# Retention values as a fifth seven-product unit, and three gate tiles ahead of the mix stage

## The chip, the cores and the metric

The kernel runs on one core of a Trainium2 chip. The metric is the time of one execution on the device in microseconds (us). One profiled execution gives the trace that is read here. The engines are named as the profile does: PE is TensorE (matrix products), DVE is VectorE, ACT is ScalarE, POOL is GpSimd, SP is SyncE, which here only issues transfers.

## The reference

Two layers run over 512 tokens of width 1024, in fp32. Each layer is a half-step SwiGLU, a mixer, and another half-step SwiGLU:

```
x = x + 0.5 * swiglu(rmsnorm(x, norm_ffn1[l]), ...)
h = rmsnorm(x, norm_mix[l]);  z = h @ w_in[l]
rq, rk, rv, rg, dq, dk, dv, g_ret, g_dil = split(z)
y_ret = retention(rq, rk, rv, rg, ...) @ w_ret_o[l]
y_dil = dilated_attention(dq, dk, dv, ...) @ w_dil_o[l]
gates = sigmoid(concat(g_ret, g_dil) + b_gate[l])
x = x + (gates[:, :1024] * y_ret + gates[:, 1024:] * y_dil) @ w_out[l]
x = x + 0.5 * swiglu(rmsnorm(x, norm_ffn2[l]), ...)
```

The change concerns `z = h @ w_in`, the projection of the mixer. Its column groups are rq and rk (512 each), rv and rg (1024 each), dq, dk and dv (1536 each), and the two gates g_ret and g_dil (1024 each).

## The kernel before

**Arithmetic.** An fp32 product is made of three faster products: each operand is split into a high part (`hi`, rounded, written by ACT) and a low part (`lo`, the rest, a subtraction on DVE), and `three` (L692 to L694) issues hi·hi, hi·lo and lo·hi. So every weight that PE uses passes a transfer on SP's queue into `raw`, an ACT copy into `ring_hi` and a DVE subtraction into `ring_lo`. PE waits for the last by the semaphore `weights_lo`. A tile of 128 by 512 results over the full depth of 1024 is 24 matmuls of 512 columns.

**The mixer of a layer** runs in this order. First the *cover*: plain blocks of z, 512 columns each, two units of weights (`cols512`) per block and four tiles of 24 matmuls per unit pair. There are three blocks, `C_DQ` (first third of dq) and two of `C_RV` (rv). While PE works on them, the other engines prepare the stage: `add_squares` on DVE (L1813, L1815) adds the squares of x, `norm_sums` on PE sums them, `norm_factor` on DVE makes the reciprocal root, `norm_spread` on PE spreads it, then DVE forms the normed input `xn` (L2308) and its sums, and `mix_operand` splits these operands (ACT L1551, DVE L2246).

Then the *stage*: the rest of dq, all of dk and dv, in four units. A unit computes 1024 columns over a 2 by 2 blocking with seven products in place of eight (`stage_product`, 24 matmuls each). DVE makes four sums of weight blocks for it (`stage_t1` to `stage_t4`, L2259, L2265, L2268), ACT and DVE split seven operands of 128x2048 (`stage_hi` L1565, `stage_lo` L2252), and the results are combined by DVE and ACT from eight PSUM banks. SP loads the weight blocks (`st_block`, L385) behind waits for earlier splits (`split_of`).

Then four *heads*, each with eight tiles of z: rq and rk, four gate tiles (two of g_ret, two of g_dil, ended by `gate_sigmoid` L1497), two tiles of rg (ended by `gate_silu` L1503). Between the matmuls of these tiles PE does the attention and retention of the head, at places written by hand in `between`: a dictionary per tile says before which of the tile's eight matmul triples a step goes. The steps that matter here: `move` (`dil_move`, L980) waits for `st_spread` of DVE (L2124); `rs(3)`, the last score product, is read by `ret_decay` (L2188); `kq(0)` to `kq(5)` (`qk_turn`, L1062) transpose the next head's q and k and are copied out by `qk_turned_copy` (`turned`, ACT L1519). `kq(2)` waits for `k_scaled` of DVE's `qk_scale` (L2237), behind `ret_decay(3)`, `qk_factors` (nine small operations) and `scores_lo(3)`. `rope` (L2167) reads the banks of the first two tiles. The results of the head before are finished in the next one by `ret_normed`, `ret_gated`, `ret_low` on DVE and `ret_out` on ACT (L1534).

Every engine runs its instructions in the order in which its own function issues them; semaphores join the engines. The *merge* and the second SwiGLU follow. In layer 0 the cover lies at 358.9 to 425.4 us of the span, the stage up to 577, the heads up to 834.5 and the merge up to 941. Layer 1 has the same order 1279.9 us later.

## Time and profile before

| | us |
|---|---|
| median of three runs | 2577.52 |
| lowest and highest | 2577.41, 2577.7 |
| the profiled execution | 2577.28 |
| its span, first to last instruction | 2575.5 |
| busy: PE | 2567.7 |
| busy: DVE | 1936.4 |
| busy: ACT | 1121.0 |

The profiled execution lasts 1.8 us longer than its span and is 0.2 us below the median. An engine's busy time is the time in which it executes an instruction. The views below are a list of PE's waits and timelines: a timeline row gives the start in us from the start of the span, the length, the engine, the line of kernel.py, the operation with output and inputs, and in brackets the idle time ahead of it and what ended that.

### The profile page before, as it was taken

How to read it: one execution, taken by the hardware profiler on the slowest of the kernel's cores; microseconds unless marked ns; L12 is line 12 of the kernel's file. 1: busy time of each engine (PE TensorE's matmuls, PEld its weight loads, DVE VectorE, ACT ScalarE, POOL GpSimd, SP SyncE). 2: the span in 40 equal slices, each digit the busy share in tenths (PEclk: the TensorE clock that was granted, in tenths of full speed). 3: DMA queues.
4: the chain of work that ended last, by engine and by line, in shares of the span. 5: the costliest groups of instructions: out<-in, count | busy, mean ns of one | idle time of the engine just before them, and what ended most of it. 6: DMA issues, size and time to landing. Idle time of an engine off the chain costs nothing.

```text
span 2575.5 us, 36835 instructions
## 1 busy us (share of the span) xinstructions
PE 2567.7 (100%) x14577; PEld 2255.3 (88%) x14577; DVE 1936.4 (75%) x2430; ACT 1121.0 (44%) x1369; POOL 128.5 (5%) x199
## 2 busy tenths in 40 slices
PE   9999999999999999999999999999999999999999
PEld 7999988888888888999989999888888888889998
DVE  8877866886776679777788777777867766797776
ACT  5433444445655234333443334454466642343332
POOL 1111000110001000000000000011100000000000
PEclk9999999999999999999999999999999999999999
DMA  5433245545443433333223332454554434333331
GB/s 183 150 124 119 66 141 191 175 161 175 138 139 115 164 103 119 103 102 98 99 83 123 98 98 74 173 178 147 172 155 139 138 128 151 115 115 98 103 107 52
DMA packets 201202, 328.98 MB, mean 128 GB/s; under 512 B 15572, under 2 KB 122497, under 8 KB 200525
## 3 DMA queue, kind: packets, MB, share of 16 engines
q1 hardware_dynamic: 186312, 286.35, 34.9%
q0 software_dynamic: 14112, 36.50, 3.9%
q10 hardware_dynamic: 646, 4.31, 0.4%
q8 instruction: 89, 1.46, 0.2%
q14 instruction: 43, 0.35, 0.0%
HBM read 289.11 MB, written 42.64 MB: 129 GB/s over the span
## 4 chain that ended last, share of the span: by engine, by line
PE 99%; DVE 0%; DMA 0%; issue 0%; ACT 0%; ACTq 0%
PE proj L692 23%; PE proj L694 23%; PE proj L693 23%; PE acc L693 9%; PE acc L692 9%; PE acc L694 9%; PE acc L1062 1%; PE acc L988 1%; PE acc L1011 0%; PE acc L970 0%; PE acc L971 0%; PE acc L972 0%; PE acc L1001 0%; PE acc L1000 0%; PE acc L765 0%; PE acc L759 0%
## 5 line engine op out<-in xcount | busy, mean ns | idle before, releaser
L692 PE MATMUL proj<-h_hi,ring_hi 128*128 128x256 f32 (+1 forms) x1632 | 553.4, 339 | 1.8 <-DVE h_lo L1791 1.8
L694 PE MATMUL proj<-h_hi,ring_lo 128*128 128x256 f32 (+1 forms) x1632 | 544.6, 334 | 0.0
L693 PE MATMUL proj<-h_lo,ring_hi 128*128 128x256 f32 (+1 forms) x1632 | 543.7, 333 | 0.0
L692 PE MATMUL proj<-y_hi,ring_hi 128*128 128x256 f32 (+1 forms) x1472 | 450.5, 306 | 0.0
L694 PE MATMUL proj<-y_hi,ring_lo 128*128 128x256 f32 (+1 forms) x1472 | 450.5, 306 | 0.0
L693 PE MATMUL proj<-y_lo,ring_hi 128*128 128x256 f32 (+1 forms) x1472 | 450.5, 306 | 0.0
L1262 ACT ACTIVATE ring_hi<-raw 128x1024 fp32r<-128x1024 f32 (+1 forms) x175 | 209.9, 1203 | 360.3 <-PE acc L694 194.6
L692 PEld LDWEIGHTS proj<-h_hi,ring_hi 128*128 128x128 f32 x1632 | 310.3, 190 | 31.4 <-DVE ring_lo L2572 2.2
L694 PEld LDWEIGHTS proj<-h_hi,ring_lo 128*128 128x128 f32 x1632 | 309.9, 190 | 31.2
L693 PEld LDWEIGHTS proj<-h_lo,ring_hi 128*128 128x128 f32 x1632 | 310.4, 190 | 27.5
L692 PEld LDWEIGHTS proj<-y_hi,ring_hi 128*128 128x128 f32 x1472 | 281.3, 191 | 12.5
L694 PEld LDWEIGHTS proj<-y_hi,ring_lo 128*128 128x128 f32 x1472 | 281.3, 191 | 12.5
L693 PEld LDWEIGHTS proj<-y_lo,ring_hi 128*128 128x128 f32 x1472 | 281.2, 191 | 12.4
L1834 DVE TENSOR_TENSOR ring_lo<-raw,ring_hi 128x1024 fp32r<-128x1024 f32 (+1 forms) x176 | 249.0, 1415 | 51.3 <-ACT ring_hi L1262 50.5
L692 PE MATMUL acc<-y_hi,ring_hi 128*128 128x512 f32 x640 | 249.3, 390 | 0.0
L693 PE MATMUL acc<-y_lo,ring_hi 128*128 128x512 f32 x640 | 249.2, 389 | 0.0
L694 PE MATMUL acc<-y_hi,ring_lo 128*128 128x512 f32 x608 | 236.5, 389 | 0.0
L1223 ACT ACTIVATE ring_hi<-raw 128x2048 fp32r<-128x2048 f32 x64 | 122.5, 1913 | 156.7 <-PE proj L694 88.5
L1783 DVE TENSOR_TENSOR ring_lo<-raw,ring_hi 128x2048 fp32r<-128x2048 f32 x64 | 146.3, 2286 | 52.0 <-ACT ring_hi L1223 51.7
L692 PEld LDWEIGHTS acc<-y_hi,ring_hi 128*128 128x128 f32 x640 | 120.2, 188 | 24.5
L693 PEld LDWEIGHTS acc<-y_lo,ring_hi 128*128 128x128 f32 x640 | 120.2, 188 | 24.3
L694 PEld LDWEIGHTS acc<-y_hi,ring_lo 128*128 128x128 f32 x608 | 114.1, 188 | 23.9
(335 smaller groups left out, 4309.6 us busy)
## 6 DMA issues: line engine op xcount, KB each, us to landing
raw<-in_w_in SPq DMA_DIRECT2D x120, 512.0 KB, 4.7
raw<-in_ffn_gate SPq DMA_DIRECT2D x88, 512.0 KB, 3.7
raw<-in_ffn_up SPq DMA_DIRECT2D x88, 512.0 KB, 4.3
raw<-in_ffn_down SPq DMA_DIRECT2D x56, 512.0 KB, 4.4
qkv_d<-work POOLq DMA_DIRECT2D x72, 256.0 KB, 2.6
work<-in_ffn_down SPq DMA_DIRECT2D x32, 512.0 KB, 5.9
xs<-qkv_d SPq DMA_DIRECT2D x24, 512.0 KB, 6.3
xs<-in_w_in SPq DMA_DIRECT2D x16, 512.0 KB, 5.2
```

Source lines behind the costliest of these rows:

```text
L692: pe.matmul(o, s_hi, m_hi, start=start, stop=False, skip_group_check=onto)
L693: pe.matmul(o, s_hi, m_lo, start=False, stop=False, skip_group_check=onto)
L694: return pe.matmul(o, s_lo, m_hi, start=False, stop=stop, skip_group_check=onto)
L988: last = pe.transpose(AB[i % 2][:, c * P:(c + 1) * P], s_t[i][:, c * P:(c + 1) * P], ident[:, :])
L1062: last = pe.transpose(bank[:, b * P:(b + 1) * P], xs[:, x, b * P:(b + 1) * P], ident[:, :])
L1223: act.activation(w_hi[u.slot][:, 0:n], raw[:, u.slot, 0:n], ACT.Copy).then_inc(weights_hi, 1)
L1262: act.activation(ring_hi[:, slot * PIECE:slot * PIECE + words], source, ACT.Copy).then_inc(weights_hi, 1)
L1783: dve.tensor_tensor(w_lo[u.slot][:, 0:n], raw[:, u.slot, 0:n], w_hi[u.slot][:, 0:n].bitcast(fp32), ALU.subtract).then_inc(weights_lo, 1)
L1834: dve.tensor_tensor(ring_lo[:, c], source, ring_hi[:, c].bitcast(fp32), ALU.subtract).then_inc(weights_lo, 1)
```

## The change

Per layer, the two `C_RV` blocks leave the cover, and rv becomes a unit of the stage, the first of now five. Three gate tiles of g_dil (`COVER_GATES`: 2, 4, 6) leave the heads 1, 2 and 3 and are computed in the cover behind the dq block, in the banks AB[2], AB[3] and PB[0]; DVE scales them (`cover_scale`), ACT takes the sigmoid (`cover_sigmoid`), POOL stores them. In matmuls of 512 columns the cover goes from 288 to 168, the stage from 672 to 840, the heads from 768 to 696. In the cover `norm_sums` moves from behind the first unit's four tiles to behind its second tile, and `norm_spread` from inside the second unit to its start. The heads 1 to 3 have seven tiles, and the tiles of all heads use banks by a table (`HEAD_BANKS`): the fifth tile of head 0 goes from PB[2] to PB[1]. The steps between the tiles are placed anew: in the heads 1 to 3, 15 matmuls lie between the last of `rs(3)` and `kq(2)`, where there were 27. On DVE `ret_normed`, `ret_gated` and `ret_low` go to the end of the head, on ACT `ret_out`, `ret_copy` and both `gate_silu` go behind `turned(5)`.

```diff
-COVER_BLOCKS, ST_UNITS = 3, 4
-ST_BASE = 2 * COVER_BLOCKS
+ST_BASE, ST_UNITS = 5, 5
+COVER_TILES = (NB, NB, 1, 1, 1)
+COVER_GATES = (2, 4, 6)
...
+HEAD_TILES = ((2, 2, 2, 2), (2, 2, 1, 2), (2, 2, 1, 2), (2, 2, 1, 2))
...
-ST_COLS = (C_DK, C_DQ + 4 * P, C_DK + 4 * P, C_DQ + 8 * P, C_DK + 8 * P, C_DV, C_DV + 4 * P, C_DV + 8 * P)
+ST_COLS = (C_RV, C_RV + 4 * P, C_DK, C_DQ + 4 * P, C_DK + 4 * P, C_DQ + 8 * P, C_DK + 8 * P, C_DV, C_DV + 4 * P, C_DV + 8 * P)
...
+        HEAD_BANKS = ((0, 1, 2, 3, 1, 2, 3, 0), (1, 2, 3, 0, 1, 2, 3), (0, 1, 2, 3, 0, 1, 2), (3, 0, 1, 2, 3, 0, 1))
...
             def cover(l):
+                item, N = unit(l, 0).index, 3 * l + 1
+                cols512(unit(l, 0), win_v, l, C_DQ, 0)
+                cols512(unit(l, 1), win_v, l, C_DQ, 4)
+                sp.dma_start(cos_r[:, :], c_cos).then_inc(rope_in, 16)
+                sp.dma_start(sin_r[:, :], c_sin).then_inc(rope_in, 16)
+                col128(unit(l, 2), win_v, l, C_GD + COVER_GATES[0] * P)
+                sp.wait_ge(ssq_added, 3 * (N + 1))
+                st_block(l, st_b22[0], 4, ST_COLS[1], b22_landed[0])
+                sp.wait_ge(norm_sum, N + 1)
+                st_block(l, st_b12[0], 0, ST_COLS[1], b12_landed)
+                col128(unit(l, 3), win_v, l, C_GD + COVER_GATES[1] * P)
+                col128(unit(l, 4), win_v, l, C_GD + COVER_GATES[2] * P)
                 split_of(item + ST_BASE - 2)
                 st_block(l, st_b11, 0, ST_COLS[0], b11_landed)
                 split_of(item + ST_BASE - 1)
...
             def cover(l):
                 N = 3 * l + 1
-                for i in range(ST_BASE):
-                    u, part, blk = unit(l, i), i % 2, i // 2
+                for part in (0, 1):
+                    u = unit(l, part)
                     begin(u)
                     for b in range(NB):
-                        if part == 0 and blk:
-                            pe.wait_ge(cover_copied, NB * (COVER_BLOCKS * l + blk - 1) + b + 1)
                         for k in range(4):
                             kt, c = 4 * part + k, k * SEQ
-                            if blk == 0 and b == 0:
+                            if b == 0:
                                 pe.wait_ge(h_lo_ready, 8 * N + kt + 1 + FREE)
                             last = three(PB[b][:, :], h_hi[:, kt, b * P:(b + 1) * P], h_lo[:, kt, b * P:(b + 1) * P],
                                          w_hi[u.slot][:, c:c + SEQ], w_lo[u.slot][:, c:c + SEQ], kt == 0, kt == KT - 1)
                         last.then_inc(tiles_done, 1)
-                        if i == 1 and b == 1:
-                            norm_spread(N)
-                    if i == 0:
-                        norm_sums(N)
+                        if part == 0 and b == 1:
+                            norm_sums(N)
+                    if part == 0:
+                        norm_spread(N)
+                for b, bank in enumerate((AB[2], AB[3], PB[0])):
+                    u = unit(l, 2 + b)
+                    begin(u)
+                    if b == 2:
+                        pe.wait_ge(cover_copied, COPIED * l + 1)
+                    tile_cols(u, bank, 0, width=P)
...
-                    between = ({2: [scores(0), scores(1)]}, {0: [scores(2), scores(3)], 1: [total]}, {2: [move]}, {},
-                               {0: [turn(0), turn(1)], 5: [turn(2), turn(3), values(0), values(1)]},
-                               {1: [values(2), values(3), near_values], 5: [rs(0)]})
-                between += ({0: [rs(1)], 1: [kq(0)], 3: [rv(0), rs(2)], 5: [kq(1)], 6: [rv(1), rs(3)]},
-                            {0: [rv(2)], 3: [rv(3), kq(2)], 4: [kq(3)], 6: [kq(4)], 7: [kq(5)]})
-                banks = PB[0:4] + PB[2:4] + PB[0:2]
-                st = 2 * ST_UNITS * l + 2 * ST_UNITS - 1 + BANK
+                    between = ({2: [scores(0), scores(1)]}, {0: [scores(2), scores(3)], 1: [total]}, {2: [move]},
+                               {2: [turn(0), turn(1)], 7: [turn(2), turn(3), values(0), values(1)]},
+                               {3: [values(2), values(3), near_values], 7: [rs(0)]})
+                if n == 0:
+                    between += ({0: [rs(1)], 1: [kq(0)], 3: [rv(0), rs(2)], 5: [kq(1)], 6: [rv(1), rs(3)]},
+                                {0: [rv(2)], 3: [rv(3), kq(2)], 4: [kq(3)], 6: [kq(4)], 7: [kq(5)]})
+                else:
+                    between += ({2: [rs(1)], 3: [kq(0)], 5: [rv(0), rs(2)], 6: [kq(1)]},
+                                {0: [rv(1), rs(3)], 2: [rv(2)], 3: [kq(2)], 4: [kq(3)], 5: [rv(3)], 6: [kq(4)], 7: [kq(5)]})
...
             def cover(l):
                 split(unit(l, 1))
-                split(unit(l, 2))
-                cover_out(l, 0, 0)
-                cover_out(l, 0, 1)
                 norm_copy(3 * l + 1)
-                cover_out(l, 0, 2)
-                cover_out(l, 0, 3)
-                split(unit(l, 3))
+                split(unit(l, 2), KT * P)
+                cover_out(l, 0)
+                cover_out(l, 1)
+                cover_out(l, 2)
                 mix_operand(l, 0)
+                cover_out(l, 3)
+                split(unit(l, 3), KT * P)
                 mix_operand(l, 1)
-                split(unit(l, 4))
-                for b in range(NB):
-                    cover_out(l, 1, b)
                 mix_operand(l, 2)
-                split(unit(l, 5))
+                split(unit(l, 4), KT * P)
                 stage_hi(l, 0, 0)
                 stage_hi(l, 0, 1)
-                for b in range(NB):
-                    cover_out(l, 2, b)
+                cover_sigmoid(l, 0)
+                cover_sigmoid(l, 1)
+                cover_sigmoid(l, 2)
...
                 squares(2, 4)
                 scores_hi(H, n, 1)
                 turned(0)
+                squares(4, 6)
+                scores_hi(H, n, 2)
+                turned(1)
+                split(at(4))
+                scores_hi(H, n, 3)
+                turned(2)
+                turned(3)
+                turned(4)
+                ret_squares(H, 0)
+                ret_squares(H, 1)
+                turned(5)
+                gate_silu(H, 0, at(3).tile)
                 if n:
                     ret_out(H - 1, n - 1, 0)
                     ret_out(H - 1, n - 1, 1)
-                squares(4, 6)
-                split(at(4))
-                scores_hi(H, n, 2)
-                turned(1)
-                scores_hi(H, n, 3)
-                gate_silu(H, 0, at(3).tile)
-                turned(2)
-                turned(3)
-                ret_squares(H, 0)
-                ret_squares(H, 1)
-                turned(4)
                 ret_copy(H, n, 0)
                 ret_copy(H, n, 1)
-                turned(5)
                 gate_silu(H, 1, at(3).tile + 1)
...
+            def cover_scale(l, b):
+                done(unit(l, 2 + b).tile)
+                dve.wait_ge(cover_stored[b], 16 * (2 * l + 1))
+                dve.tensor_tensor(cover_gate[b], (AB[2], AB[3], PB[0])[b][:, :], r_b[:, :], ALU.mult).then_inc(sxn_ready, 1)
...
                 add_squares(N)
                 split(unit(l, 1))
                 norm_factor(N)
-                split(unit(l, 2))
                 dve.wait_ge(r_ready, N + 1)
-                for m in range(KT):
-                    dve.scalar_tensor_tensor(xn[:, m, :], xs[:, m, :], pars[l][:, R_N[1] + m:R_N[1] + m + 1], r_b[:, :],
-                                             ALU.mult, ALU.mult).then_inc(sxn_ready, 1)
-                dve.wait_ge(sxn_ready, KT * (l + 1))
-                dve.tensor_tensor(s_acc, xn21, xn22, ALU.add).then_inc(sum_ready, 1)
-                split(unit(l, 3))
+                normed(NB, KT)
+                split(unit(l, 2), KT * P)
+                normed(0, NB)
+                dve.wait_ge(sxn_ready, SXN * l + KT)
+                dve.wait_ge(x_spilled, 16 * (l + 1))
+                dve.tensor_tensor(s_sum, xn21, xn22, ALU.add).then_inc(sum_ready, 1)
                 dve.tensor_tensor(s_diff, xn11, xn21, ALU.subtract).then_inc(sum_ready, 1)
                 mix_operand(l, 0)
                 dve.wait_ge(sum_ready, 4 * l + 1)
-                dve.tensor_tensor(s_acc, xn11, s_acc, ALU.subtract).then_inc(sum_ready, 1)
+                dve.tensor_tensor(s_sum, xn11, s_sum, ALU.subtract).then_inc(sum_ready, 1)
+                split(unit(l, 3), KT * P)
                 mix_operand(l, 1)
-                split(unit(l, 4))
                 mix_operand(l, 2)
                 dve.wait_ge(sum_ready, 4 * l + 3)
-                dve.tensor_tensor(s_acc, xn12, s_acc, ALU.add).then_inc(sum_ready, 1)
-                split(unit(l, 5))
+                dve.tensor_tensor(s_sum, xn12, s_sum, ALU.add).then_inc(sum_ready, 1)
+                split(unit(l, 4), KT * P)
                 stage_t1(l, 0)
                 stage_t3(l, 0)
                 stage_lo(l, 0, 0)
+                cover_scale(l, 0)
+                cover_scale(l, 1)
                 stage_t2(l, 0)
                 stage_lo(l, 0, 1)
+                cover_scale(l, 2)
...
                     ret_factor(H - 1)
-                    ret_normed(H - 1)
                 split(at(3))
-                if n:
-                    ret_gated(H - 1)
                 dil_out(H, n)
...
-                if n:
-                    ret_low(H - 1, n - 1)
                 ret_decay(H, 2)
                 reduce(4)
                 scores_lo(H, n, 2)
                 reduce(5)
-                split(at(4))
                 ret_decay(H, 3)
                 if more:
                     qk_factors(H + 1)
                 scores_lo(H, n, 3)
                 if more:
                     qk_scale(H + 1)
+                split(at(4))
+                if n:
+                    ret_normed(H - 1)
+                    ret_gated(H - 1)
+                    ret_low(H - 1, n - 1)
```

In the cover DVE's order around the stage's first operands is this. `y_lo` and `h_lo` are the low parts of mix operands, `ring_lo` those of weights; `raw<-xs,raw` and its like are the weight sums. Before:

```order
L2321 TENSOR_TENSOR work<-work 128x1024
L1783 TENSOR_TENSOR ring_lo<-raw,ring_hi 128x2048
L2259 TENSOR_TENSOR raw<-xs,raw 128x2048
L2265 TENSOR_TENSOR xs<-xs 128x2048
L2252 TENSOR_TENSOR ring_lo<-raw,ring_hi 128x2048
L2268 TENSOR_TENSOR raw<-raw,xs 128x2048
L2252 TENSOR_TENSOR ring_lo<-xs,ring_hi 128x2048
L2252 TENSOR_TENSOR ring_lo<-raw,ring_hi 128x2048
L2246 TENSOR_TENSOR h_lo<-work,h_hi 128x4x256 x2
L2246 TENSOR_TENSOR y_lo<-work,y_hi 128x1024
L2246 TENSOR_TENSOR h_lo<-work,h_hi 128x4x256 x2
L2252 TENSOR_TENSOR ring_lo<-raw,ring_hi 128x2048
```

Of the change (L2322 is `mix_operand`, L2328 `stage_lo`, L2335 `stage_t1`, L2341 `stage_t3`, L2344 `stage_t2`, L2379 `cover_scale`):

```order
L2335 TENSOR_TENSOR raw<-work,raw 128x2048
L2341 TENSOR_TENSOR work<-work 128x2048
L2328 TENSOR_TENSOR ring_lo<-raw,ring_hi 128x2048
L2379 TENSOR_TENSOR xs<-acc,r_b 128x512 x2
L2344 TENSOR_TENSOR raw<-raw,work 128x2048
L2328 TENSOR_TENSOR ring_lo<-work,ring_hi 128x2048
L2379 TENSOR_TENSOR xs<-proj,r_b 128x512
L2328 TENSOR_TENSOR ring_lo<-raw,ring_hi 128x2048
L2322 TENSOR_TENSOR h_lo<-work,h_hi 128x4x256 x2
L2322 TENSOR_TENSOR y_lo<-xs,y_hi 128x1024
L2322 TENSOR_TENSOR h_lo<-work,h_hi 128x4x256 x2
L2328 TENSOR_TENSOR ring_lo<-raw,ring_hi 128x2048
```

The sums and splits keep their order among themselves; three scalings of gate tiles (L2379) now lie between them.

At the end of head 1 ACT's order is as follows, from the first `gate_silu` (L1503) to the first exponential of head 2 (L1446). L1519 is `turned`, here (2) to (5), L1524 `ret_squares`, L1529 `ret_copy`, L1223 a split. Before:

```order
L1503 ACT_TABLE_LOAD
L1503 ACTIVATE work<-proj 128x512
L1519 ACTIVATE xs<-acc,gqs 128x4x8x16
L1519 ACTIVATE xs<-acc,params 128x4x8x16
L1524 ACTIVATE work<-acc 128x512 x2
L1519 ACTIVATE xs<-acc,params 128x512
L1529 ACTIVATE work<-acc,params 128x512 x2
L1519 ACTIVATE xs<-acc,params 128x512
L1503 ACTIVATE work<-proj 128x512
L1223 ACTIVATE ring_hi<-raw 128x2048
L1446 ACT_TABLE_LOAD
L1446 ACTIVATE work,raw<-work,raw 128x128
```

Of the change, from `turned(3)` on (L1578 `turned`, L1583 `ret_squares`, L1562 `gate_silu`, L1593 `ret_out`, L1588 `ret_copy`, L1502 the exponentials):

```order
L1578 ACTIVATE xs<-acc,params 128x4x8x16
L1578 ACTIVATE xs<-acc,params 128x512
L1583 ACTIVATE work<-acc 128x512 x2
L1578 ACTIVATE xs<-acc,params 128x512
L1562 ACT_TABLE_LOAD
L1562 ACTIVATE work<-proj 128x512
L1593 ACTIVATE y_hi<-work 128x512 x2
L1588 ACTIVATE work<-acc,params 128x512 x2
L1562 ACTIVATE work<-proj 128x512
L1279 ACTIVATE ring_hi<-raw 128x2048
L1502 ACT_TABLE_LOAD
L1502 ACTIVATE work,raw<-work,raw 128x128
```

The table load with the first `gate_silu`, and the two `ret_out`, which stood ahead of `turned(2)`, now stand behind `turned(5)`, and so do the two `ret_copy`; `ret_squares` went from ahead of `turned(4)` to behind it. `ret_out` is followed on DVE by `ret_low`, for which `ret_copy` waits.

## Rows read from the trace of the kernel before

**Rows 1.** All waits of PE: who waited for whom, us in total, times, longest.
```profile
PE acc L1205 <- DVE ones_r L2525: 2.8, 1, 2.8
PE proj L692 <- DVE h_lo L1791: 1.8, 1, 1.8
```

**Rows 2.** Span and mean granted TensorE clock of the core.
```profile
core 0: 2575.5 us, clock 1.000
```

**Rows 3.** Timeline of PE, layer 0, cover: start us, us, engine, line, operation.
```profile
358.90 0.39 PE L692 MATMUL proj<-ring_hi,h_hi 128*128 128x512 f32 x1
...
364.34 0.39 PE L692 MATMUL proj<-ring_hi,h_hi 128*128 128x512 f32 x1
```

**Rows 4.** Timeline of DVE, layer 0, start of the cover.
```profile
364.83 0.69 DVE L1815 TENSOR_TENSOR work<-work 128x512 f32<-128x512 f32 x1
```

**Rows 5.** Timeline of DVE, layer 0, cover.
```profile
388.58 1.22 DVE L2246 TENSOR_TENSOR y_lo<-work,y_hi 128x1024 fp32r<-128x1024 f32 x1
389.72 1.22 DVE L2316 TENSOR_TENSOR work<-work 128x1024 f32<-128x1024 f32 x1
...
417.42 2.28 DVE L2268 TENSOR_TENSOR raw<-raw,xs 128x2048 f32<-128x2048 f32 x1
419.62 2.28 DVE L2252 TENSOR_TENSOR ring_lo<-xs,ring_hi 128x2048 fp32r<-128x2048 f32 x1
```

**Rows 6.** Timeline of ACT, layer 0, cover.
```profile
405.05 1.05 ACT L1551 ACTIVATE y_hi<-work 128x1024 fp32r<-128x1024 f32 x1
406.00 1.91 ACT L1223 ACTIVATE ring_hi<-raw 128x2048 fp32r<-128x2048 f32 x1
```

**Rows 7.** Tile raw, 399 to 424 us: its loads' times to landing.
```profile
DMA to landing us min/median/max: 3.7/4.4/4.9
```

**Rows 8.** Issues of line 385: duration ns min/median/max, first and last start.
```profile
L385 SPq DMA_DIRECT2D raw<-in_w_in x32: 367/419/510, 399.2 to 1803.3; - x32
```

**Rows 9.** Timeline of PE, head 0 of layer 0, start of its fifth tile.
```profile
607.38 0.47 PE L692 MATMUL proj<-h_hi,ring_hi 128*128 128x512 f32 x1
607.69 0.39 PE L693 MATMUL proj<-h_lo,ring_hi 128*128 128x512 f32 x1
```

**Rows 10.** Timeline of DVE, head 0 of layer 0.
```profile
608.23 0.68 DVE L2167 TENSOR_TENSOR work<-proj,cos_sin 128x512 f32<-128x512 f32 x1
```

**Rows 11.** Timeline of ACT, head 0 of layer 0.
```profile
605.25 1.28 ACT L1497 ACT_TABLE_LOAD   x1
606.55 0.69 ACT L1497 ACTIVATE r_b<-proj,params 128x512 f32<-128x512 f32 x1
```

**Rows 12.** Timeline of PE, end of head 1 of layer 0.
```profile
693.88 0.39 PE L694 MATMUL acc<-ring_lo 128*128 128x512 f32 x1
...
704.79 0.60 PE L1062 MATMUL acc<-ident,xs 128*128 128x128 f32 x4
```

**Rows 13.** Timeline of DVE, end of head 1 of layer 0.
```profile
694.31 0.69 DVE L2188 SCALAR_TENSOR_TENSOR work<-acc,raw 128x512 f32<-128x512 f32 x1 [0.48 <-PE acc L694]
...
699.73 0.68 DVE L2188 SCALAR_TENSOR_TENSOR work<-acc,raw 128x512 f32<-128x512 f32 x1
...
702.88 1.22 DVE L2237 TENSOR_TENSOR xs<-xs,q_rqk 128x1024 f32<-128x1024 f32 x1
```

**Rows 14.** Timeline of ACT, end of head 1 and start of head 2.
```profile
710.12 0.69 ACT L1519 ACTIVATE xs<-acc,params 128x512 f32<-128x512 f32 x1
710.69 0.61 ACT L1503 ACTIVATE work<-proj 128x512 f32<-128x512 f32 x1
...
714.81 0.40 ACT L1446 ACTIVATE work<-work,raw 128x128 f32<-128x128 f32 x1 [0.41 <-DVE raw L2118]
...
716.63 0.51 ACT L1446 ACTIVATE work<-work,raw 128x256 f32<-128x256 f32 x1 [0.84 <-DVE raw L2118]
```

**Rows 15.** Timeline of DVE, start of head 2.
```profile
724.90 0.23 DVE L2124 TENSOR_TENSOR raw<-raw 128x64 f32<-128x64 f32 x1 [0.64 <-ACT work L1446]
```

**Rows 16.** Timeline of PE, start of head 2.
```profile
726.47 0.30 PE L980 MATMUL acc<-raw 128*128 128x32 f32 x2
```

More of the change, by code:

```diff
@@ L109, in piece_tile @@
 def piece_tile(layer, u, j):
-    return layer * TILES_LAYER + FFN_TILES + NB * ST_BASE + 2 * (PROD * u + j)
+    return layer * TILES_LAYER + FFN_TILES + sum(COVER_TILES) + 2 * (PROD * u + j)
 def ffn_item(layer, f):
@@ L376, in two_cols128, with col128 @@
                          (v[:, :, :, P:2 * P], w[:, ds(layer, 1), :, ds(col1, P)])])
+            def col128(u, w, layer, col):
+                v = slot(u, KT * P).rearrange("p o (k c) -> p o k c", c=P)
+                load(u, [(v[:, :, k:k + 4, :], w[:, ds(layer, 1), k:k + 4, ds(col, P)]) for k in (0, 4)])
             def cols512(u, w, layer, col, k0=0):
@@ L1502, in gate_silu @@
                     act.wait_ge(ret_y, 4 * H)
-                act.activation(silu[:, e, :], PB[e][:, :], ACT.Silu).then_inc(silu_ready, 1)
+                n = H % RET_HEADS
+                bank = head_bank(n, 2 + len(head_gates(n)) + e)
+                act.activation(silu[:, e, :], bank[:, :], ACT.Silu).then_inc(silu_ready, 1)
             def qk_square(H, x):
@@ L1647, in heads @@
                     split(at(2))
+                    dil_exps(H, 2)
+                    dil_exps(H, 3)
+                    swap_halves(H, 1, at(0).tile + 1)
+                    rope_hi(H, 0)
+                    dil_factors(H)
+                    gate_sigmoid(l, n, 0)
+                    gate_sigmoid(l, n, 1)
+                    dil_copy(H, 0)
+                    dil_copy(H, 1)
+                    rope_hi(H, 1)
+                    split(at(3))
+                    dil_copy(H, 2)
+                    dil_copy(H, 3)
+                    dil_out(H, n)
+                    squares(0, 2)
+                    gate_sigmoid(l, n, 2)
+                    scores_hi(H, n, 0)
+                    gate_sigmoid(l, n, 3)
                 else:
```

220 lines of the change are left out of this document (122 added, 98 removed).

## The prediction

> **What bounds the kernel now.** The first view to read is the list of PE's waits [rows 1]. It has two entries in the whole program, 2.8 us at the start and 1.8 us a little later: in every other place PE goes from one matmul to the next. The other engines have much idle time, but none of it is PE's. So two rules hold for this kernel: a matmul that goes away is worth its whole slot, and a wait of PE that comes new costs its whole length. The second view is PE's timeline, for the slot: 24 matmuls of 512 columns lie between 358.90 and 364.34 [rows 3], so one is 5.44 / 24 = 0.2267 us. The third is the timelines of DVE and ACT at the places where the change lets PE arrive earlier or lets its supplier start later.
>
> **What the change removes.** A layer's mixer has 288 + 672 + 768 = 1728 such matmuls in cover, stage and heads before and 168 + 840 + 696 = 1704 after. The 24 fewer are 24 × 0.2267 = 5.44 us in a layer, 10.88 us in the two. The small products of attention and retention stay. The weights, loads and splits that go with the matmuls lie beside PE and cost nothing unless PE comes to wait for them, which is the rest of the sum. It goes through five places where PE's new position and its supplier's new time come close. Each is worked out for layer 0; layer 1 has the same order.
>
> **1. `norm_sums` in the cover.** It waits for the sum of squares. It was issued behind four tiles and now is behind two, that is at 364.34 [rows 3], since the cover starts at 358.90 as before. DVE's last addition ends at 364.83 + 0.69 = 365.52 [rows 4]; a hand-over from PE to DVE takes 694.31 − (693.88 + 0.39) = 0.04 [rows 12, 13], and I take it for the other pairs. DVE's work ahead of it is unchanged. Wait: 365.56 − 364.34 = 1.2 us. Behind it are all of the cover's matmuls.
>
> **2. The fourth product of the stage's first unit.** From the last matmul of the dq block, PE now has three gate tiles and three products ahead of it, 144 matmuls, 32.64 us. Its weights come out of a chain that starts when that block ends, about 0.2 us after PE has gone on (a matmul lasts 0.39 and the next starts 0.23 after it). ACT evicts the block's last tile (0.57, the step between two such evictions in [rows 14]), splits a gate unit of 1024 (1.05 [rows 6]), DVE completes the split (1.22 [rows 5]); only then SP may issue the two loads of the next weight block. Their landing takes 3.7 to 4.9 [rows 7], and the second is issued 0.42 later [rows 8]: 4.1 to 5.3, I take 5.0, since both must land. DVE then does a sum of 2.28, and one operation after the other of 2048 columns at a step of 419.62 − 417.42 = 2.20 [rows 5]: the second sum, a split, (two scalings, 2 × 0.60), the third sum, a split, a scaling of 0.69. ACT follows with a sigmoid, 0.57, and a split of 1.91 [rows 6]. DVE has 2.20 for that one, five operands at 389.72 − 388.58 = 1.14, and 2.29 for the fourth split. The sum is 0.2 + 0.57 + 1.05 + 1.22 + 5.0 + 2.28 + 2.20 + 2.20 + 1.20 + 2.20 + 2.20 + 0.69 + 0.57 + 1.91 + 2.20 + 5.70 + 2.29 = 33.7, with eight hand-overs of 0.04 34.0. Wait: 34.0 − 32.6 = 1.4 us, between 0.5 and 1.8 by the landing times and a hand-over more or less. Before, one and a half blocks more covered this chain.
>
> **3. The fifth tile of head 0.** It goes to the bank PB[1], which `rope` of the second tile must have read. PE is there at 607.38 [rows 9]; `rope`'s reading runs from 608.23 to 608.91 [rows 10]. Wait: 608.95 − 607.38 = 1.6 us. The DVE work ahead of `rope` is not moved, so it doesn't come earlier.
>
> **4. `kq(2)` in heads 1 and 2.** It waits for `k_scaled`, whose chain starts with the last matmul of `rs(3)`. DVE takes that product up 694.31 − 693.88 = 0.43 after its start [rows 12, 13]; from there to the end of `qk_scale` it is 702.88 + 1.22 − 699.73 = 4.37, back to back. With a hand-over 4.84 us. Between them PE now has 15 matmuls besides the last of `rs(3)` itself, 16 × 0.2267 = 3.63. Wait: 1.2 us, in two heads. Before, 27 lay between, and `kq(2)` came at 704.79, after the chain's end at 704.10 [rows 12, 13].
>
> **5. `move` in heads 2 and 3.** Before, `st_spread` came at 724.90 + 0.23 + 0.04 = 725.17 and PE at 726.47 [rows 15, 16], so 1.3 us are to spare. PE's work from the last turns of a head to `move` is of the same length, so what counts is what ACT has more to do between `turned(4)` and the exponentials. These are a table load of 1.28 [rows 11], two `ret_squares`, one `gate_silu` and two `ret_out`, five steps of 0.5 to 0.57 [rows 14], and the wait of `ret_copy` for DVE's second `ret_low`, 0.69 and two hand-overs: 4.6 us. A part is taken up where ACT waited for DVE before, 0.41 and 0.84 [rows 14]; DVE's next steps leave perhaps 0.5 more, which I estimate from nothing to 1.0. Wait: 4.6 − 1.25 − 0.5 − 1.3 = 1.5 us, from 1.1 to 2.0, in two heads. At the end of head 0 there is no `ret_out` and no `ret_low`, some 1.8 less, and `move` of head 1 is in time.
>
> At this place the Trainium skill speaks against the change: "ScalarE: Activation LUTs", section "What ACT_TABLE_LOAD costs", has a drain of some 1.38 us behind the load, 2.66 in all. The trace does not show it: the load at 605.25 lasts 1.28, and the sigmoid starts at 606.55 [rows 11]. By the page's figure each of the four waits at `move` would be an estimated 1.38 longer; I go by the row.
>
> Ahead of these, the moved parts that I cost at nothing have cover: the seven more DVE splits and the combinations of the fifth unit are for seven more products, and the units behind the first, of the same load, give PE no wait [rows 1]; the new sigmoid's table load in the cover is on ACT while DVE does the third sum; POOL's three more stores in the cover have all of the stage before they are read.
>
> **The sum.** A matmul behind such a wait starts its stream with a step of some 0.3 in place of 0.23 (607.38 to 607.69 behind other products [rows 9]), so I add 0.1 to each wait of 2 to 5, six in a layer. Waits: 1.2 + 1.4 + 1.6 + 2 × 1.2 + 2 × 1.5 + 6 × 0.1 = 10.2 us. Less 5.44 this is +4.8 in a layer, +9.6 in two. The profiled execution took 2577.28 us (2575.5 of span and 1.8 around it), 0.2 below the median of 2577.52, so I forecast 2577.3 + 9.6 = **2587 us**. The low ends of all terms (1.0, 0.5, 1.4, 2 × 1.1, 2 × 1.1, nothing added) give 7.3 and 2581; the high ends (1.4, 1.8, 1.8, 2 × 1.4, 2 × 2.0, 0.6) give 12.4 and 2591.
>
> **The rivals.**
>
> *The waits don't add up (chance 0.08, faster).* If PE's first wait delayed it against DVE and ACT for good, the later chains would find it late and only the longest wait of a layer would count: 1.6 − 5.44 = −3.8, two layers 2569.7. What decides is whether the chains run by themselves or are released by PE. It ends faster as soon as a layer's waits are under 5.44 − 2.6 = 2.8 us. For it speaks DVE's idle time. Against it: each of the chains 2 to 5 starts at a PE product (the end of a block, `rs(3)`, the last turns), so a late PE makes its chain late. With none of the waits there it would be 2577.3 − 10.9 = 2566.4.
>
> *The heads' chains are shorter (chance 0.12, same).* If the places 4 and 5 cost nothing, because ACT's extra steps fit where it idles in the head, the waits are 1.2 + 1.5 + 1.7 = 4.4, and the time is 2577.3 + 2 × (4.4 − 5.44) = 2575; with half of their waits 2581. Against it: at 4 the DVE operations follow each other without a gap.
>
> *The clock falls (chance 0.04, slower).* PE's granted clock is 1.000 over the whole span, the higher of its two levels (2.4 GHz), although PE waited 2.8 and 1.8 us in it [rows 1, 2]. None of the new waits is longer than these, but there are fourteen. If one tile of 24 matmuls behind each ran at the lower level (1.2 GHz), it would cost 5.4 us more each time, and the time would be 2587 + 14 × 5.4 = 2663. The Trainium skill, "TensorE: Matmul & The Clock Gate", section "HAM oscillation — how this bites in real kernels", describes a kernel in which idle gaps brought the lower level back again and again; by the trace so far, gaps of this length did not.
>
> *The table load drains (chance 0.03, slower).* If the sets' change held ACT back as much again as the load itself, the four waits at `move` would each be about 1.3 longer, 2587 + 5.2 = 2592. Rows 11 speak against it.
>
> **How the numbers follow.** The forecast case has the remaining 0.73. Its range is 2581 to 2591. To hold the time 8 times in 10 the range takes in a part of the second rival and the fourth: 2578 to 2592. A measurement tells 0.2%, 5.2 us, from no change. Slower than 2582.7 are most of the forecast case (0.71) and the last two rivals, 0.78; within it the second rival and the lowest end of the forecast, 0.14; faster than 2572.3 the first rival, 0.08.
>
> **What would show it.** PE's list of waits should have `norm_sums` on the sum of squares (1.2), a stage product on a DVE split of 2048 (1.4), a tile of head 0 on `rope` (1.6), `kq(2)` on `qk_scale` (1.2, twice) and `move` on `st_spread` (1.5, twice), each in both layers, some 19 us together, and PE's busy time should fall by 11. The prediction is wrong where the entries are missing, where the same entry is much longer in one layer than in the other, where a transfer is named as the releaser of the fourth product, or where the granted clock is under 1.

## The result, and the profile after

| | before | changed |
|---|---|---|
| median, us | 2577.47 | 2602.31 |
| lowest and highest | 2577.34, 2577.7 | 2602.15, 2604.23 |
| ratio, 95% interval | | 1.0098 [1.008, 1.0115] |
| span of the profiled execution | 2575.5 | 2600.3 |
| PE busy | 2567.7 | 2569.0 |
| mean granted clock of TensorE | 1.000 | 0.997 |

The change makes the kernel 24.8 us slower. 2587 was forecast, with a range of 2578 to 2592. The direction held, the size did not.

The page of the profile after has the busy time of each engine with its share and its instructions (PEld is TensorE's loading of weights), and the shares of the chain that ended last:

```profile
PE 2569.0 (99%) x14529; PEld 2250.7 (87%) x14529; DVE 1986.2 (76%) x2476; ACT 1132.4 (44%) x1375; POOL 129.0 (5%) x199
...
PE 91%; DVE 5%; ACT 3%; issue 1%; DMA 0%; SPq 0%; ACTq 0%; DVEq 0%
```

The chain was 99% PE before; now 8% of it is DVE and ACT: at PE's new waits the chain goes back through the work of these engines that PE waited for. PE's busy time did not fall by 10.9 us but rose by 1.3, with 48 matmuls less. The list of PE's waits (who waited for whom, us in total, times, longest us) answers to [rows 1]:

```profile
PE acc L1026 <- DVE raw L2200: 9.4, 4, 2.3
PE acc L1108 <- DVE xs L2313: 4.3, 4, 1.1
PE proj L730 <- DVE work L2243: 3.1, 2, 1.5
PE acc L1261 <- DVE ones_r L2613: 2.8, 1, 2.8
PE proj L730 <- DVE ring_lo L2328: 2.6, 2, 1.3
PE acc L805 <- DVE work L1891: 2.1, 2, 1.1
PE proj L730 <- DVE h_lo L1867: 1.8, 1, 1.8
PE proj L730 <- DVE ring_lo L1859: 1.7, 2, 0.8
```

The two entries of before, on `ones_r` and on `h_lo` at the start, are still there. The other six are new, 23.2 us together. All five forecast places are among them: `move` (L1026), `kq(2)` (L1108), the fifth tile of head 0 (L730 on L2243), the fourth product (on L2328), `norm_sums` (L805). The sixth, on L1859, was not forecast: a weight split of the merge, in both layers.

Behind some of these waits PE runs slower. The timeline of PE at `move` of head 2 in layer 0:

```profile
738.08 0.39 PE L732 MATMUL proj<-h_hi,ring_lo 128*128 128x512 f32 x1
740.81 0.61 PE L1026 MATMUL acc<-raw 128*128 128x32 f32 x2 [2.35 <-DVE raw L2200]
...
741.65 0.77 PE L730 MATMUL proj<-h_hi,ring_hi 128*128 128x512 f32 x1
...
742.65 0.63 PE L732 MATMUL proj<-h_hi,ring_lo 128*128 128x512 f32 x1
743.08 0.63 PE L730 MATMUL proj<-h_hi,ring_hi 128*128 128x512 f32 x1
...
746.92 0.56 PE L730 MATMUL proj<-h_hi,ring_hi 128*128 128x512 f32 x1
747.32 0.40 PE L731 MATMUL proj<-h_lo,ring_hi 128*128 128x512 f32 x1
```

The wait is 2.35 us. Behind it the matmuls of 512 columns start 0.43 apart and last 0.63, where 0.23 and 0.39 are usual [rows 3], for some 6 us. The windows around that place (stretch and its length, busy us of PE, PEld, DVE, ACT and POOL with their instructions, granted clock, DMA share, GB/s) show the clock:

```profile
740.00:744.00 4.00, 3.19 (x10) 2.74 (x11) 3.38 (x10) 3.67 (x8) 0.00 (x0) 0.55 0.87 228
744.00:748.00 4.00, 4.00 (x12) 3.14 (x11) 3.86 (x15) 1.05 (x1) 0.00 (x0) 0.59 0.51 150
748.00:752.00 4.00, 4.00 (x23) 3.36 (x22) 2.14 (x5) 2.25 (x4) 0.56 (x1) 1.00 0.62 182
```

It is granted at 0.55 and 0.59 in the first two, so at the lower of the two levels (1.2 GHz) for most of the time, and at 1.00 in the last. Such stretches stand at four places of this execution: behind `move` at 741 (13 matmuls of 512 columns), 2034 (7) and 2098 (8), and behind `norm_sums` at 1658 (7). The windows around the last three:

```profile
1658.00:1663.00 5.00, 5.00 (x16) 3.96 (x16) 2.56 (x10) 0.00 (x0) 0.00 (x0) 0.66 0.98 333
2033.00:2038.00 5.00, 4.20 (x14) 3.47 (x15) 4.34 (x13) 4.67 (x8) 0.00 (x0) 0.66 0.72 188
2098.00:2103.00 5.00, 4.70 (x16) 3.83 (x17) 4.72 (x16) 4.24 (x6) 0.00 (x0) 0.66 0.01 2
```

So 24.8 us are made of three parts. The matmuls that went are −10.9. The waits are 23.2, and the 16 of them cost 0.24 each more, 3.8; this price is measured in run g1 below at `move`, and taken for all. The rest, 24.8 + 10.9 − 27.0 = 8.7 us, is the lower clock. The windows give the same size by another way: what the clock lacks of 1.00, times the length, is 4 × 0.45 + 4 × 0.41 = 3.4 us at 741 and 5 × 0.34 = 1.7 at each of the other three, 8.5 in all.

### The profile page after: what moved, and what is told of

It is laid out like the page before. It is cut to its first block, busy times and chain, and to the rows that moved or that the text cites. A ratio compares the mean times of both kernels' runs of the same rounds, so it can differ in the third digit from the quotient of the medians.

```text
span 2600.3 us, 36837 instructions
## 1 busy us (share of the span) xinstructions
PE 2569.0 (99%) x14529; PEld 2250.7 (87%) x14529; DVE 1986.2 (76%) x2476; ACT 1132.4 (44%) x1375; POOL 129.0 (5%) x199
## 4 chain that ended last, share of the span: by engine, by line
PE 91%; DVE 5%; ACT 3%; issue 1%; DMA 0%; SPq 0%; ACTq 0%; DVEq 0%
PE proj L730 20%; PE proj L732 20%; PE proj L731 20%; PE acc L730 9%; PE acc L732 9%; PE acc L731 9%; PE acc L1108 1%; DVE ring_lo L2328 1%; PE acc L1034 1%; ACT ring_hi L1279 0%; PE acc L1057 0%; ACT work L1502 0%; DVE h_lo L1867 0%; DVE y_lo L2295 0%; DVE h_lo L2322 0%
## 5 line engine op out<-in xcount | busy, mean ns | idle before, releaser
L730 PE MATMUL proj<-h_hi,ring_hi 128*128 128x256 f32 (+1 forms) x1600 | 543.3, 340 | 4.9 <-DVE work L2243 3.1
L732 PE MATMUL proj<-h_hi,ring_lo 128*128 128x256 f32 (+1 forms) x1600 | 534.1, 334 | 0.0
L731 PE MATMUL proj<-h_lo,ring_hi 128*128 128x256 f32 (+1 forms) x1600 | 533.5, 333 | 0.0
L730 PE MATMUL proj<-y_hi,ring_hi 128*128 128x256 f32 (+1 forms) x1472 | 450.7, 306 | 1.7 <-DVE ring_lo L1859 1.7
L730 PEld LDWEIGHTS proj<-h_hi,ring_hi 128*128 128x128 f32 x1600 | 305.8, 191 | 34.0 <-issue 4.1
L730 PEld LDWEIGHTS proj<-y_hi,ring_hi 128*128 128x128 f32 x1472 | 281.2, 191 | 15.0 <-DVE ring_lo L1859 2.5
L730 PE MATMUL acc<-y_hi,ring_hi 128*128 128x512 f32 x640 | 249.3, 390 | 0.0
L1279 ACT ACTIVATE ring_hi<-raw 128x2048 fp32r<-128x2048 f32 (+1 forms) x62 | 108.4, 1748 | 122.8 <-PE proj L732 57.9
L1628 ACT ACTIVATE ring_hi<-raw 128x2048 fp32r<-128x2048 f32 x50 | 95.6, 1917 | 141.4 <-PE acc L732 80.7
L1859 DVE TENSOR_TENSOR ring_lo<-raw,ring_hi 128x2048 fp32r<-128x2048 f32 (+1 forms) x62 | 129.0, 2081 | 34.3 <-ACT ring_hi L1279 34.3
L2328 DVE TENSOR_TENSOR ring_lo<-raw,ring_hi 128x2048 fp32r<-128x2048 f32 x50 | 114.3, 2289 | 53.5 <-ACT ring_hi L1628 53.5
L730 PEld LDWEIGHTS acc<-y_hi,ring_hi 128*128 128x128 f32 x640 | 120.2, 188 | 24.5
```

The costliest lines, as they stand in the source:

```text
L730: pe.matmul(o, s_hi, m_hi, start=start, stop=False, skip_group_check=onto)
L731: pe.matmul(o, s_hi, m_lo, start=False, stop=False, skip_group_check=onto)
L732: return pe.matmul(o, s_lo, m_hi, start=False, stop=stop, skip_group_check=onto)
L1279: act.activation(w_hi[u.slot][:, 0:n], raw[:, u.slot, 0:n], ACT.Copy).then_inc(weights_hi, 1)
L1628: act.activation(ring_hi[:, c:c + 2048], source, ACT.Copy).then_inc(weights_hi, 1)
L1859: dve.tensor_tensor(w_lo[u.slot][:, 0:n], raw[:, u.slot, 0:n], w_hi[u.slot][:, 0:n].bitcast(fp32), ALU.subtract).then_inc(weights_lo, 1)
```

## The experiments

Two theories stood against each other after this. The first: everything beside the 48 matmuls is waits at the six places and the lower clock that they bring on. The second: the fifth unit, or the load of the whole program, has a cost of its own, in the clock or elsewhere, and the waits explain only a part. Experiments e1 to e6 take waits out of the changed kernel, one place at a time or several together; g1 to g3 and h1 put them into the kernel before.

| run | median, us | ratio to before, 95% interval |
|---|---|---|
| e1_act_order | 2584.02 | 1.0023 [1.0013, 1.0033] |
| e2_rs3_first | 2593.35 | 1.0060 [1.0044, 1.0077] |
| e3_sums_later | 2597.85 | 1.0079 [1.0062, 1.0096] |
| e4_four_undone | 2569.67 | 0.9970 [0.9958, 0.9981] |
| e5_sigmoid_later | 2596.57 | 1.0075 [1.0060, 1.0091] |
| e6_all_waits_undone | 2566.27 | 0.9957 [0.9943, 0.9970] |
| g1_move_4_earlier | 2586.80 | 1.0036 [1.0022, 1.0050] |
| g2_move_5_earlier | 2599.71 | 1.0083 [1.0066, 1.0100] |
| g3_move_7_earlier | 2612.41 | 1.0135 [1.0118, 1.0152] |
| h1_sums_early_in_before | 2581.84 | 1.0019 [1.0010, 1.0029] |

**e1: most of the heads' end in the old order.** On DVE `ret_normed` and `ret_gated` go back around `split(at(3))` and `ret_low` behind `reduce(3)`; on ACT `ret_out` and the first `gate_silu` go back. `ret_copy` stays behind `turned(5)`, though the expectation names it among what moves, and `ret_squares` stays too:

```diff
                 turned(0)
+                if n:
+                    ret_out(H - 1, n - 1, 0)
+                    ret_out(H - 1, n - 1, 1)
                 squares(4, 6)
...
+                gate_silu(H, 0, at(3).tile)
                 turned(2)
...
                 turned(5)
-                gate_silu(H, 0, at(3).tile)
-                if n:
-                    ret_out(H - 1, n - 1, 0)
-                    ret_out(H - 1, n - 1, 1)
                 ret_copy(H, n, 0)
```

> The changed kernel, but in the heads the end of a head has the order of the kernel before: ret_normed, ret_gated, ret_low (DVE) and ret_out, ret_copy, the first gate_silu (ACT) stand where they stood. Theory: the time over the prediction comes from PE's waits, which are longer at move than forecast, and from stretches at the lower clock behind waits. Then the four waits at move (9.4 us) and the two in the merge (1.7) go, with 0.25 each for the start of the stream behind them, and so do the three stretches at the lower clock behind move (28 matmuls, about 5.6): 2602.3 - 18.2 = 2584. Rival: the lower clock is not brought on by these waits and stays somewhere else: 2590. Rival: the wait at move is not ACT's order but something later in DVE's chain: no change, 2602.

It took 2584.02. The waits at `move` and in the merge are gone from PE's list; those at `kq(2)` (4.3) and in head 0 (3.1) have the lengths of the changed kernel. That the time meets the forecast to the tenth is in part luck: the forecast left one stretch at the lower clock, and the profiled execution (2584.42) has two, behind `norm_sums` in both layers.

What had held `move` is seen by laying the two timelines of ACT side by side, from `turned(5)` to the first exponential. In the changed kernel:

```profile
721.76 0.70 ACT L1578 ACTIVATE xs<-acc,params 128x512 f32<-128x512 f32 x1
722.48 1.28 ACT L1562 ACT_TABLE_LOAD   x1
723.77 0.60 ACT L1562 ACTIVATE work<-proj 128x512 f32<-128x512 f32 x1
724.27 1.14 ACT L1593 ACTIVATE y_hi<-work 128x512 fp32r<-128x512 f32 x2
726.47 1.27 ACT L1588 ACTIVATE work<-acc,params 128x512 f32<-128x512 f32 x2 [1.06 <-DVE y_lo L2295]
...
731.35 0.40 ACT L1502 ACTIVATE work<-work,raw 128x128 f32<-128x128 f32 x1
```

In e1:

```profile
723.22 0.70 ACT L1578 ACTIVATE xs<-acc,params 128x512 f32<-128x512 f32 x1
723.79 1.29 ACT L1588 ACTIVATE work<-acc,params 128x512 f32<-128x512 f32 x2
...
727.38 1.28 ACT L1502 ACT_TABLE_LOAD   x1
728.68 0.40 ACT L1502 ACTIVATE work<-work,raw 128x128 f32<-128x128 f32 x1
```

In the changed kernel 9.59 us lie between them (721.76 to 731.35), in e1 5.46 (723.22 to 728.68), in the kernel before 4.69 [rows 14]. What the changed kernel has more than e1 is what the rows name: the table load and `gate_silu` (722.48 to 724.27), two `ret_out` and 1.06 of waiting for `ret_low`; two `ret_copy` come on top against the kernel before. No run parts these from each other, their shares are read from the rows. The load lasts 1.28 and `gate_silu` starts 1.29 after its start, so no drain stands behind it. In this the trace goes on to differ from the Trainium skill, "ScalarE: Activation LUTs", section "What ACT_TABLE_LOAD costs", which puts about 1.38 us of drain behind the load.

**e2: `rs(3)` ahead of `rv(1)` in the heads 1 to 3.**

```diff
-                            {0: [rv(1), rs(3)], 2: [rv(2)], 3: [kq(2)], 4: [kq(3)], 5: [rv(3)], 6: [kq(4)], 7: [kq(5)]})
+                            {0: [rs(3), rv(1)], 2: [rv(2)], 3: [kq(2)], 4: [kq(3)], 5: [rv(3)], 6: [kq(4)], 7: [kq(5)]})
```

> The changed kernel, but in the heads 1 to 3 rs(3) is issued ahead of rv(1) and not behind it, so that 21 matmuls lie between it and kq(2) in place of 15. Theory: the chain behind rs(3) is of fixed length (about 4.8 us), so the four waits at kq(2) (4.3 us) go, with 0.25 each: 2602.3 - 5.3 = 2597. Rival: the chain is held by something else than rs(3), the wait stays: 2602.

It took 2593.35, and the four waits at `kq(2)` are gone. That is 9 us less and not 5.3. The profiled execution had four stretches at the lower clock, as the changed kernel, at the same mean clock of 0.997, and took 2596.86, which is the forecast; the other three executions took 2592.5 to 2594.1 at a mean clock of 0.998 or 0.999, so with fewer or shorter stretches. The wait was worth what it was said to be, and the number of stretches varies from execution to execution.

**e3: `norm_sums` behind three tiles.**

```diff
-                        if part == 0 and b == 1:
+                        if part == 0 and b == 2:
```

> The changed kernel, but norm_sums comes behind three tiles of the first unit in place of two. Theory: the two waits (2.1 us) go, with 0.25 each, and the stretch at the lower clock behind the one of layer 1 (7 matmuls, 1.4) with them: 2598. Rival: the clock falls elsewhere for it: 2600. Rival: the norm comes later for it, and the wait at the fourth product grows by what is gained: 2602.

It took 2597.85, as forecast. The two waits and the stretch at 1658 are gone, and the wait at the fourth product is 1.30 and 1.55 where it was 1.27 and 1.34, so little of what was gained can have come back there. Three stretches are left, all at `move`.

**e4: e1, e2, e3 and an earlier reading of the bank in head 0.** The last is this, on DVE:

```diff
+                if n == 0:
+                    rope_first(H, 1)
                 dil_combine(H)
                 for i in range(NB):
                     dil_scale(H, i)
-                rope(H, 1)
+                rope(H, 1, n > 0)
```

`rope_first` is the first operation of `rope`, the one that reads the bank.

> The changed kernel with e1, e2 and e3 together, and in head 0 the first operation of the second rope (the one that reads the bank) ahead of dil_combine and dil_scale. Left of the found waits is the one at the fourth product (1.3, twice). Theory (the matmuls that went are worth their 10.9 us, all the rest is waits and their clock): 2577.3 - 10.9 + 2 x 1.6 = 2570, granted clock 1.000. Rival (the fifth unit costs something that no wait shows): 2575 or more with the waits gone.

2569.67, clock 1.000. PE's list, whole:

```profile
PE acc L1261 <- DVE ones_r L2620: 2.8, 1, 2.8
PE proj L730 <- DVE ring_lo L2332: 2.7, 2, 1.4
PE proj L730 <- DVE h_lo L1867: 0.6, 1, 0.6
```

Only the fourth product is left of the new waits.

**e5: the third sigmoid behind the third weight split.** In ACT's cover `cover_sigmoid(l, 2)` goes, and in its stage:

```diff
                 stage_hi(l, u, 2)
                 if u == 0:
+                    cover_sigmoid(l, 2)
                     for n in range(3, OPERANDS):
```

> The changed kernel, but the sigmoid of the third gate tile (cover_sigmoid 2) is issued on ACT behind the first unit's third weight split (stage_hi 2) in place of ahead of it. Theory: the chain to the fourth product then goes through DVE alone from the second split on and is shorter by the sigmoid, that split and two hand-overs (about 2.6), so the two waits there (2.6 us) go, with 0.25 each: 2602.3 - 3.1 = 2599. Rival: DVE is the bound of the first unit, and the wait turns up at a later product of it: 2602.

2596.57. The wait at the fourth product is gone and comes up at no later product, so DVE alone keeps pace in the first unit. The time is under the forecast: the profiled execution has three stretches at the lower clock, of 7 or 8 matmuls, where the changed kernel's had four, one of them of 13.

**e6: all of them together.**

> The changed kernel with the edits of e1, e2, e3, e5 and the moved rope operation of e4. Theory: no wait of PE is left behind the first 12 us, and what is left of the change are the 48 matmuls: 2577.5 - 10.9 = 2566.6, clock 1.000. Rival (the fifth unit has a cost beside waits): 2569 or more.

2566.27, with 0.07 us between the fastest and the slowest execution, and faster than both kernels. PE on the page, and its list of waits:

```profile
PE 2556.8 (100%) x14529; PEld 2246.7 (88%) x14529; DVE 1983.8 (77%) x2476; ACT 1131.6 (44%) x1375; POOL 128.4 (5%) x199
```

```profile
PE acc L1261 <- DVE ones_r L2620: 2.8, 1, 2.8
PE proj L730 <- DVE h_lo L1867: 1.6, 1, 1.6
```

PE's busy time is 2567.7 − 2556.8 = 10.9 us under that of before, which is 48 × 0.2267 to the tenth. The second theory falls: with the waits undone the fifth unit costs nothing beside its matmuls. Against e4, which differs by the edit of e5 alone, e6 is 3.4 us faster: two waits of 1.3 and 1.4, and 0.3 to 0.4 more for each. So the 0.24 of g1 may be low for other places, and the share of the waits somewhat larger.

**g1 to g3: the kernel before, with `move` of the heads 1 to 3 earlier.** It is one entry of `between`; g1 has 6, g2 has 5, g3 has 3:

```diff
-                    between = ({2: [scores(0), scores(1)]}, {0: [scores(2), scores(3)], 1: [total]}, {2: [move]}, {},
+                    between = ({2: [scores(0), scores(1)]}, {0: [scores(2), scores(3)], 1: [total], 6: [move]}, {}, {},
```

> The kernel before, with move of the heads 1 to 3 issued four matmul triples earlier (ahead of the seventh triple of the second tile); nothing else is changed. It had 1.3 us to spare and comes 2.7 earlier, so PE waits 1.4 us in six places and the work is the same. Theory (a wait costs its length and about 0.25 more; the clock falls behind longer waits): 2577.3 + 6 x 1.65 = 2587, clock 1.000 or one fall. Rival (the clock falls by PE's mean load, not by a single wait): 2587 and no fall in any of the three.

> The same with move five triples earlier: waits of 2.1 us in six places. Theory: 2577.3 + 6 x 2.35 = 2591.4, and behind some of them a stretch at the lower clock, some 2 us each, so 2594 to 2603. Rival (no falls by single waits): 2591.

> The same with move seven triples earlier: waits of 3.4 us in six places. Theory: 2577.3 + 6 x 3.65 = 2599, and a stretch at the lower clock behind nearly all, 2609 to 2615. Rival (no falls by single waits): 2599.

They took 2586.80, 2599.71 and 2612.41. PE's wait at `move` in the three, in this order:

```profile
PE acc L980 <- DVE raw L2124: 7.9, 6, 1.3
```

```profile
PE acc L980 <- DVE raw L2124: 11.9, 6, 2.0
```

```profile
PE acc L980 <- DVE raw L2124: 20.1, 6, 3.4
```

In g1 the clock is 1.000. Its 2586.80 − 2577.53 = 9.27 us are six waits of 1.31 and 0.24 more for each; this is the price of a wait used above. A part of it is only the way of counting: the list counts from the end of the last matmul, which lasts 0.39, while the next one would have started 0.23 after its start [rows 3], so 0.16 of lost time is in no entry. The other 0.08 is the step of 0.31 with which the stream starts anew. In g2 five of the six waits have a stretch at the lower clock behind them, in g3 all six. The windows of g2 behind its first three waits (at 661, 728 and 796):

```profile
660.00:664.00 4.00, 2.93 (x15) 2.52 (x16) 3.00 (x10) 0.71 (x5) 0.00 (x0) 1.00 1.18 295
664.00:668.00 4.00, 4.00 (x20) 3.30 (x19) 0.12 (x2) 3.91 (x6) 0.00 (x0) 1.00 0.35 100
727.00:731.00 4.00, 3.21 (x10) 2.76 (x11) 2.88 (x9) 0.36 (x2) 0.00 (x0) 0.61 1.19 293
796.00:802.00 6.00, 5.86 (x16) 4.83 (x17) 2.69 (x9) 0.74 (x1) 0.00 (x0) 0.51 0.00 0
```

Behind the first wait the clock stays at 1.00, behind the second and third it falls to the lower level, with the same wait ahead. In g3, 34.9 us less the waits (20.1 + 6 × 0.24) leave 13.3, 2.2 us on the mean for each of the six stretches. So the lower clock is brought on by single waits; the kernel before, with PE's load all else the same, shows it too.

**h1: the kernel before, with `norm_sums` behind two tiles.**

```diff
+                        if i == 0 and b == 1:
+                            norm_sums(N)
                         if i == 1 and b == 1:
                             norm_spread(N)
-                    if i == 0:
-                        norm_sums(N)
```

> The kernel before, with norm_sums of the cover behind two tiles of the first unit in place of four, as in the changed kernel; nothing else is changed. Two waits of 1.1 us. In the runs so far the clock fell behind four of six such waits, and behind none of those of 1.3 and 1.5 us at other places. Theory (what is issued behind the wait counts: eight products of one column): 2577.5 + 2 x 1.3 = 2580, and one or two stretches at the lower clock of 7 or 8 matmuls (1.6 us each): 2581.5 to 2583.5, mean clock 0.999. Rival (it was the changed kernel's other work around it): 2580, clock 1.000.

2581.84, clock 0.999. Of ten executions six took 2581.5 to 2581.9 and four 2583.3 to 2583.6. The profiled one, of the faster kind, has one stretch. Its PE timeline in layer 1:

```profile
1646.95 1.05 PE L759 MATMUL acc<-ones,work 128*128 128x1 f32 x8 [1.07 <-DVE work L1815]
1647.87 0.48 PE L692 MATMUL proj<-ring_hi,h_hi 128*128 128x512 f32 x1
...
1648.67 0.63 PE L692 MATMUL proj<-ring_hi,h_hi 128*128 128x512 f32 x1
1649.09 0.63 PE L693 MATMUL proj<-ring_lo,h_hi 128*128 128x512 f32 x1
```

The wait is 1.07, the eight one-column products behind it take 0.92, and from the fourth matmul after them the steps are 0.42. Had neither wait a stretch behind it, the time would be 2577.43 + 2 × (1.07 + 0.24) = 2580.1. One stretch adds 1.7, a second would account for the slower executions. So the clock falls here without the changed kernel's other work, and the rival (2580 at a clock of 1.000) is out; that the eight products are the reason is not shown.

## Why the prediction was wrong

**The frame held.** A matmul that goes is worth its slot, and a new wait costs in full: e6 shows the first to a tenth of a us. The five places were the right ones:

| place | forecast | measured | times |
|---|---|---|---|
| 1, `norm_sums` | 1.2 | 1.07 | 2 |
| 2, fourth product | 1.4 | 1.27, 1.34 | 2 |
| 3, fifth tile of head 0 | 1.6 | 1.54 | 2 |
| 4, `kq(2)` | 1.2 | 1.07 | 4 |
| 5, `move` | 1.5 | 2.35 | 4 |
| merge, not forecast | 0 | 0.83 | 2 |
| more for each wait | 0.1 (2 to 5) | 0.24 (at `move`, g1) | |

The measured column has the lengths of PE's list, which start 0.16 later than the forecast's (see g1). With them added the places 1 to 4 are 1.2, 1.4 and 1.5, 1.7, and 1.2, so these four sums came out, and the 0.1 for the restart is the 0.08 found. The longest chain, at the fourth product, holds step by step: PE leaves the dq block at 383.98, the loads are issued from 387.10, the first sum starts at 392.13 (5.0 for both loads), and the last split ends at 418.00, 34.0 us after PE left the block, as forecast.

Single removals (e1, e2, e3, e5) show the places 1, 2, 4, 5 and the merge to be what was named. Place 3 was undone only together with others, in e4, where its wait went.

**The step that failed is the third rival, "the clock falls".** It had a chance of 0.04, on the ground that the clock was 1.000 although PE had waited 2.8 and 1.8 us at the program's start [rows 1, 2], and "None of the new waits is longer than these". The waits inside the running program did bring the lower level: behind 2.35 us at `move` in 12 of 16 cases (the changed kernel, e2, e3 and e5), behind 2.0 us in five of six (g2), behind 3.35 in all six (g3). This is 8.7 of the 15.3 us by which the forecast was short.

The ground itself was misread. Behind the wait of 2.8 us the kernel before runs fifteen matmuls of 512 columns (`WARM`). Two windows of them, with the mean length of one in ns, from 2.8 to 6.2 us and from 6.5 to 7.5:

```profile
L1205 PE MATMUL acc<-ones_r 128*128 128x512 f32 x8 | 3.7, 642 | 2.8 <-DVE ones_r L2525 2.8
L1205 PE MATMUL acc<-ones_r 128*128 128x512 f32 x6 | 1.5, 381 | 0.0
```

The first eight start some 0.43 apart and last 0.64 on the mean, as in the stretches at the lower clock; the later six have the usual length. The views give 1.00 for these first microseconds too, but the trace's record of the clock begins only at 6.3 us, where the matmuls become short. So the trace of before did not show that a wait of 2.8 us leaves the clock alone; whether this slow stretch comes from the wait or from the program's start, no run tells. Only the 1.8 us were followed by the usual pace (so were 2.1 us at the same place in e1 and e2). The rival's own price was too high: it reckoned with 14 stretches of 5.4 us, and there were four, of 3.4 and three times 1.7. The Trainium skill, "TensorE: Matmul & The Clock Gate", section "HAM oscillation — how this bites in real kernels", describes idle gaps that bring the lower level back; its gaps are transfer waits of some 3 to 5 us, repeated at every step. That single waits of 2.0 us do it, and not every time, is what g2 shows.

**The waits are the other 6.6 us.** Forecast were 2 × 10.2 = 20.4, measured 27.0; 4.0 of the difference is at `move`, 2.1 in the merge. Term 5 was forecast at 1.5 and measured 2.35, above the 2.0 that was its high end. By the forecast's own way of counting it is 2.4, in this way. From `turned(5)` to the first exponential ACT takes 9.59 − 4.69 = 4.90 more, although the 0.41 of idle time went [rows 14], so the work added is 5.3 where the forecast had 4.6; 0.3 of the difference is the wait for `ret_low`, 1.06 where 0.77 was counted. From there to the end of `dil_spread`, before 714.81 to 725.13 [rows 14, 15], 0.96 were taken up, where the forecast had 0.84 and half a us. The end after is this row of DVE:

```profile
740.48 0.23 DVE L2200 TENSOR_TENSOR raw<-raw 128x64 f32<-128x64 f32 x1 [0.64 <-ACT work L1502]
```

So it is 740.71 − 731.35 = 9.36 against 10.32. That gives 4.90 − 0.96 − 1.3 = 2.6, and `turned(5)` itself comes 0.2 earlier against PE, since the two `ret_squares` ahead of it take 0.95, where the two `ret_copy` took 1.14.

**The merge's wait was overlooked**: the same order at the heads' end delays ACT and DVE at the end of head 3, and the next weight split with them. e1 undoes most of that order and nothing else, and the two waits of 0.83 go. I had followed the order only up to the next `move`.

**The other rivals.** "The waits don't add up" and "the heads' chains are shorter" fell: e1, e2, e3 and e5 each took out their own waits, and the others stayed at their lengths. "The table load drains" fell too: in e1 as in the changed kernel the next activation starts 1.3 us after the load's start. What the prediction named as its signs was met in the list of waits, missed in PE's busy time (what the matmuls take longer at the lower clock counts as busy), and the sign of failure that it named last, a granted clock under 1, is the one that came.

## What to carry to other kernels

Where PE is busy all the time, a change that removes matmuls is worth what it removes only if no order around it lets PE arrive early: here 10.9 us were there to be had, and 35.7 were lost to orders that four small moves and one split operation of `rope` put right (e6, 0.43% faster than before). Follow each moved step to the next place where PE waits for that engine, and then to the one after it. And put a wait of 2 us inside a running stream of matmuls down at nearly twice its length (22.2 us for six of them in g2), since the clock may fall behind it. To learn what a wait does to the clock, read the steps of the matmuls behind it, and not only the granted clock of a view.
